# Two blocks of weights interleaved unit by unit while their turned operand is made

## The reference

```
h = rms_norm(x, norm_gain[i])            # first block; the even layer projects mem as well,
kv = einsum('bmd,dc->bmc', mem_n, w_kv)  # and keys and values of mem are two blocks of its columns
...
for l in range(DEPTH):                   # second block
    u = rms_norm_2(h, norm_pre_mix[l])
    p = (u @ w_in[l]).astype(jnp.float32)
    p_ret, p_hgrn, p_ml, p_rw = split_cols_2(p, GROUP_COLS)
    ...
    h = h + rms_norm_2(mixed, norm_post_mix[l])
    u = rms_norm_2(h, norm_pre_ffn[l])
    ffn = (jax.nn.silu(u @ w_ffn_gate[l]) * (u @ w_ffn_up[l])) @ w_ffn_down[l]
    h = h + rms_norm_2(ffn, norm_post_ffn[l])
```

## Time and profile before

| | us |
|---|---|
| median of 3 runs | 3916.73 (3912.31 to 3918.07) |
| span of the profiled execution | 3913.3 |
| TensorE busy | 3798.5 |
| VectorE busy | 2256.0 |
| ScalarE busy | 1795.6 |
| mean granted clock of TensorE | 0.985 |

### The profile page before, as it was taken

The page is one execution under the profiler, slowest core; times in us unless marked ns, Lnnn a source line. Parts: engine busy times, 40 slices in busy tenths (PEclk is TensorE's granted clock), DMA queues, the critical chain, the costliest instruction groups (busy, mean ns, idle before and its releaser), DMA issues.

```text
span 3913.3 us, 49190 instructions
## 1 busy us (share of the span) xinstructions
PE 3798.5 (97%) x19948; PEld 3204.6 (82%) x19948; DVE 2256.0 (58%) x3532; ACT 1795.6 (46%) x2519; POOL 104.5 (3%) x61
## 2 busy tenths in 40 slices
PE   8999999999999999989999999999999989999998
PEld 7886778787898897778888888988987778888887
DVE  5665666675555746764454444566656664445444
ACT  6454545445454424544444444545325454444443
POOL 0000000000010000000000000010000000000000
PEclk9999999999999999999999999999999999999999
DMA  7655546563554405446666655544225446666654
GB/s 239 184 167 147 145 135 179 158 188 101 182 165 135 122 26 159 146 146 190 191 188 189 200 194 193 178 125 143 63 78 153 152 140 189 192 189 189 201 193 169
DMA packets 341426, 628.34 MB, mean 161 GB/s; under 512 B 21088, under 2 KB 63024, under 8 KB 340432
## 3 DMA queue, kind: packets, MB, share of 16 engines
q1 hardware_dynamic: 331920, 611.53, 51.7%
q10 hardware_dynamic: 9280, 13.69, 1.1%
HBM read 623.04 MB, written 2.10 MB: 160 GB/s over the span
## 4 chain that ended last, share of the span: by engine, by line
PE 88%; DVE 6%; ACT 3%; POOL 1%; issue 1%; DMA 1%; SPq 0%; ACTq 0%; DVEq 0%; POOLq 0%
PE bank L621 74%; DVE weights_low L527 2%; PE bank L745 1%; PE bank L1320 1%; PE bank L1417 1%; PE bank L2524 1%; PE bank L2538 1%; PE bank L2131 1%; PE bank L2537 1%; ACT weights_high L514 1%; PE bank L600 1%; PE bank L1400 1%; POOL stat L706 0%; PE bank L1323 0%; POOL arena L706 0%
## 5 line engine op out<-in xcount | busy, mean ns | idle before, releaser
L527 DVE TENSOR_TENSOR weights_low<-weights,weights_high 128x1024 fp32r<-128x1024 f32 (+3 forms) x1176 | 1393.7, 1195 | 979.0 <-ACT weights_high L514 967.7
L514 ACT ACTIVATE weights_high<-weights 128x1024 fp32r<-128x1024 f32 (+3 forms) x1176 | 1206.9, 1030 | 1341.2 <-PE bank L621 1284.1
L621 PE MATMUL bank<-weights_high,x_high 128*128 128x512 f32 (+3 forms) x2816 | 1116.7, 397 | 21.4 <-DVE weights_low L527 9.7
L621 PE MATMUL bank<-weights_low,x_high 128*128 128x512 f32 (+3 forms) x2816 | 1086.3, 386 | 0.0
L621 PE MATMUL bank<-weights_high,x_low 128*128 128x512 f32 (+3 forms) x2816 | 1086.0, 386 | 0.0
L621 PEld LDWEIGHTS bank<-weights_high,x_high 128*128 128x128 f32 x2816 | 536.0, 190 | 135.4 <-DVE weights_low L527 17.2
L621 PEld LDWEIGHTS bank<-weights_low,x_high 128*128 128x128 f32 x2816 | 535.0, 190 | 101.8
L621 PEld LDWEIGHTS bank<-weights_high,x_low 128*128 128x128 f32 x2816 | 536.3, 190 | 93.1
L621 PE MATMUL bank<-x_high,weights_high 128*128 128x256 f32 x960 | 279.6, 291 | 12.2 <-DVE arena L650 6.0
L621 PE MATMUL bank<-weights_high,y_high 128*128 128x512 f32 (+1 forms) x672 | 266.2, 396 | 8.7 <-DVE weights_low L527 6.5
L621 PE MATMUL bank<-weights_high,ff_high 128*128 128x512 f32 x704 | 274.0, 389 | 0.0
(11 more groups left out here) (385 smaller groups left out, 3618.8 us busy)
## 6 DMA issues: line engine op xcount, KB each, us to landing
weights<-in_w_in_dram SPq DMA_DIRECT2D x208, 512.0 KB, 3.6
weights<-in_w_ffn_gate_dram SPq DMA_DIRECT2D x176, 512.0 KB, 3.7
weights<-in_w_ffn_up_dram SPq DMA_DIRECT2D x176, 512.0 KB, 3.6
weights<-in_w_ffn_down_dram SPq DMA_DIRECT2D x176, 512.0 KB, 3.6
weights<-in_w_out_dram SPq DMA_DIRECT2D x128, 512.0 KB, 3.6
weights<-in_even_w_in_dram SPq DMA_DIRECT2D x88, 512.0 KB, 3.6
weights<-in_odd_w_in_dram SPq DMA_DIRECT2D x80, 512.0 KB, 3.6
weights<-in_mem_w_kv_dram SPq DMA_DIRECT2D x32, 512.0 KB, 4.2
```

The costliest lines, as they stand in the source:

```text
L514: self.high_mark[g] = self.high_split.count(act.ran(nc.scalar.activation(high, raw, ACT.Copy)), act.clock)
L527: self.low_mark[g] = self.low_split.count(dve.ran(nc.vector.tensor_tensor(low, raw, high.bitcast(F32), ALU.subtract)), dve.clock)
L621: ins = pe.ran(nc.tensor.matmul(out, l, r, start=(u + c + x + y == 0), stop=(u == blk.n - 1 and c == UNIT - 1 and y == 1)))
```

## The change

`side_by_side(one, two)` takes the units of the two blocks added last and interleaves them: one's unit 0, two's unit 0, one's unit 1 and so on. It is called for mem0.k with mem0.v, o.i0 with o.i1, and in both layers of the second block for hgq with hgf0. For this the four chunks of hgf become two blocks of two chunks: hgf0 on banks 6 and 7, hgf1 on banks 4 and 5. Turns for these operands then use banks 4 and 5 alone (in `turn_x` with `spread`, and in `post_norm` after "down"). `hgrn` waits for three blocks in place of two. What is computed and every matmul is the same.

```diff
--- before.py
+++ after.py
@@ -485,6 +485,13 @@
         self.pair = 0
         self.add(Block(name, "features", self.by_unit(W, 0, D, col, chunks * P), D // (UNIT * P), chunks * P,
                        tuple(range(bank0, bank0 + chunks)), evac, AT, 0, None, scale))
+
+    def side_by_side(self, one, two):
+
+        n = self.blocks[one].n
+        first, second = self.units[-2 * n:-n], self.units[-n:]
+        assert {b.name for b, u in first} == {one} and {b.name for b, u in second} == {two}
+        self.units[-2 * n:] = [unit for both in zip(first, second) for unit in both]
 
     def load(self, g):
 
@@ -908,6 +915,8 @@
             for k, dst in ((0, self.mk[i]), (1, self.memv[i])):
                 self.tokens(f"mem{i}.{'kv'[k]}", self.hT_mem, A["mem_w_kv"][i], 0, D, k * 512, 512,
                             self.scaled_out(lambda t, dst=dst: dst[:, t, :], sc["mem"]), scale=sc["mem"])
+            if i == 0:
+                self.side_by_side("mem0.k", "mem0.v")
         self.plan_even()
         self.plan_odd()
         self.layers = [self.plan_layer(l) for l in range(2)]
@@ -978,6 +987,8 @@
                         self.scaled_out(lambda t: po[:, t, col:col + width], rs, ((0, width, func),)), scale=rs)
         for k in range(3):
             part(f"i{k}", 2560 + k * 368, 368)
+            if k == 1:
+                self.side_by_side("o.i0", "o.i1")
         part("k", O_["c_k"], 512)
         part("v", O_["c_v"], 512)
         for k in range(3):
@@ -1087,7 +1098,7 @@
                 yield
             self.ready([f"{name}{nb}"], self.pe)
             for c in (4 * nb, 4 * nb + 2):
-                self.turn(AT, c, self.x_chunk, 4 + c // 2 % 4, gain)
+                self.turn(AT, c, self.x_chunk, 4 + c // 2 % (2 if spread else 4), gain)
                 if nb < 3:
                     yield
         self.rms_of(self.squares, rs)
@@ -1739,8 +1750,10 @@
             dst = rows(HG + 2048 + k * 1024)
             self.tokens(n + "hg" + "ig"[k], L.hT, W, 0, D, (6 + k) * GW, GW,
                         self.scaled_out(lambda t, dst=dst: dst[:, t, :], L.pre, ((0, GW, func),)), scale=L.pre)
-        for k in range(2):
-            self.features(n + "hg" + "qf"[k], L.hT, W, 4 * GW + k * GW, 4, self.features_out(lambda j, k=k: room(HG, 4 * k + j), L.pre), 4 * k, scale=L.pre)
+        for name, col, chunks, at, bank in (("hgq", 0, 4, 0, 0), ("hgf0", GW, 2, 4, 6), ("hgf1", GW + 2 * P, 2, 6, 4)):
+            self.features(n + name, L.hT, W, 4 * GW + col, chunks, self.features_out(lambda j, at=at: room(HG, at + j), L.pre), bank, scale=L.pre)
+            if name == "hgf0":
+                self.side_by_side(n + "hgq", n + "hgf0")
         rwkv(0)
         rwkv(1)
         hgrn(0, ACT.Copy)
@@ -1891,7 +1904,7 @@
             if c == 0:
                 self.turn_first(AT, c, self.x_chunk, gain)
             else:
-                self.turn(AT, c, self.x_chunk, 4 + (c // 2 + 1) % 4, gain)
+                self.turn(AT, c, self.x_chunk, 4 + (c // 2 + 1) % (4 if "out" in name else 2), gain)
             if c == 0:
                 marks[2] = update(0, 2 * P, TILE)
                 if "out" in name:
@@ -2048,8 +2061,9 @@
         act.wait_ge(*[m for m in self.blocks["o.out_dsa3" if l == 0 else "0.down3"].done])
         for i, name in enumerate(("const_halves", "const_halves_T")):
             self.aux(masks[:, :, i, :], self.A[name].rearrange("p (l n) -> p l n", l=LEVELS))
-        yield from self.need(nm + "hgq", nm + "hgf")
-        self.ready([nm + "hgq", nm + "hgf"], act, dve)
+        names = [nm + "hgq", nm + "hgf0", nm + "hgf1"]
+        yield from self.need(*names)
+        self.ready(names, act, dve)
         yield from self.meet()
         landed = self.aux(gain, self.A["hgrn_norm_w_2"][l].partition_broadcast(P))
         over = lambda a: a.unsqueeze(2).broadcast_to([P, 4, S])
```

## The result

The changed kernel takes 3925.64 us (median of 6 runs, 3918.16 to 3930.57), the kernel before 3913.78 in the same job: a ratio of 1.0029, interval 1.0020 to 1.0039. It is slower, by 11.9 us. A later job with ten more runs of it gave 1.0027 (1.0018 to 1.0036). The forecast was 3917.6 in a range of 3904 to 3931, with 0.66 on "no difference" and 0.18 on slower. Its "no difference" reached 7.8 us to either side; 11.9 us lies outside it, on the slower side.

What follows compares the result with a forecast made beforehand. The prediction took TensorE, busy 3798.5 of 3913.3 us, as the bound. Its sum was 3916.7 - 0.1 (interleaving) + 1.0 (later hgrn chain) = 3917.6 us, all other terms 0; range 3904 to 3931 for 8 in 10.

Steps and rivals of the forecast that it cites:

- no difference: Case for the whole kernel: measured time within 7.8 us of no change, 3908.9 to 3924.6; chance 0.66.
- the four places: Where the change interleaves: TensorE already full while turns and stream alternate; gain taken 0.1 us, bound 1.7.
- A and B: Start (mem0.k, mem0.v) and first block of the odd layer (o.i0); gain taken 0 and 0.1 us.
- C: Start of layer 0 of the second block (hgq, hgf); interleaving gains 0 there.
- D: Start of layer 1 of the second block (hgq, hgf); interleaving gains 0 there.
- D's 4.1 and 0.7 us: Layer 1's start: TensorE waits for the first updated x and first low half; claimed to stay, gain 0.
- C's 0.9: Layer 0's start: TensorE's 0.91 us wait for an addition into x that frees bank 0; claimed to stay.
- Turns on two banks ... Taken 0: Layer 0 and 1 starts: a bank frees before the turn needing it; cost 0, up to 1 us possible.
- The chain behind the narrow units: hgrn's ACT chain behind hgf1 starts late through transfer waits; cost taken 1.0 us, 0 to 2.8 both layers.
- The slower rival: Behind hgf1, ACT's transfer waits become TensorE's through hgrn's chain: 13.5 us slower, 3930.2; chance 0.18.
- The faster rival: The shifted schedule frees the 3.41 us evacuation wait at 2750.95: 9.4 us gained, 3907.3, perhaps 3901.0; chance 0.16.
- The base: Starting time of the sum: 3916.7 us, the runs' median, 3.4 above the profiled span, carried unchanged.

Runs made afterwards that it cites:

- A and B alone: The kernel before with only mem0.k/mem0.v and o.i0/o.i1 interleaved; 3914.87 us, ratio 1.0001 (0.9992 to 1.0010).
- the change with its harm at C repaired: The changed kernel with three banks for the turns and the row of factors in layer 0 laid out later; 3916.22 us, ratio 1.0004 (0.9994 to 1.0015).
- two banks alone: The kernel before with turns in layers 0 and 1 on banks 4 and 5 in place of four, nothing interleaved or split; 3917.60 us, ratio 1.0012.
- second profile of the changed kernel: Another profiled execution of the changed kernel, same program; span 3921.9 us, against 3916.8 in the first profile.
- narrow units alone: The kernel before with hgf in two blocks of two chunks, nothing interleaved, four banks for the turns; 3916.01 us, ratio 1.0006 (0.9995 to 1.0016).
- three banks: The changed kernel with hgf0 cut to one chunk and hgf1 of three, leaving three banks for the turns; 3918.13 us, ratio 1.0008.
- layer 1 alone: The kernel before with only the change's layer 1 part: hgq and hgf0 interleaved, two banks for the turns; 3915.78 us, ratio 1.0004 (0.9996 to 1.0013).
- the late row: The changed kernel with layer 0's row of factors not laid out before the factor is expected, 27 weight matmuls ahead in place of 3; 3920.51 us, ratio 1.0012.
- early row: The kernel before with layer 0's row of factors laid out right behind the last turn, no weight matmul between; 3919.14 us, ratio 1.0008 (1.0000 to 1.0017).

## Why the prediction was right and wrong

- **The time lies in the range, the case doesn't.** 0.66 stood on a difference of less than 7.8 us, and it is 11.9. The range held because it was drawn wide for both rivals; neither made the difference.
- **That TensorE has nothing to fill at the four places** held. A and B alone give 1.0001, and the change with its harm at C repaired gains nothing. D's 4.1 and 0.7 us stayed, and C's 0.9 (now 0.7) nearly so, as the sum had them.
- **"Turns on two banks ... Taken 0" was the step that failed.** It rested on "each turn is followed by at least one unit". At C that wasn't so even in the kernel before, where only three matmuls of a unit's 24 stand between the last turns:

```profile
1060.10 0.60 PE L745 MATMUL bank<-const,x_residual 128*128 128x128 f32 x4
...
1060.89 0.60 PE L745 MATMUL bank<-const,x_residual 128*128 128x128 f32 x4
...
1061.68 1.04 PE L745 MATMUL bank<-const,x_residual 128*128 128x128 f32 x8
```

  With this order two banks alone cost a wait of 0.92 us, inside the 1 us that I allowed. But the order is computed anew from expected times, and the changed kernel has four turns in a row; its waits are 1.8. At D, where an update of x stands between turns, the wait for a bank is 0.2, though the row waits there too (0.2 in the change, 0.5 with two banks alone).
- **What hangs behind those turns had no term at all.** The row of factors was covered by 39 weight matmuls. With 3 in their place it costs 2.5 us of waiting, and the lower clock takes 2.6 more. Undoing this one thing gives 5.2 us back in C; making it in the kernel before costs 5.2. The sum never asks what the present order covers.
- **The chain behind the narrow units**, 1.0 us taken, at most 2.8, was right in kind in both layers. The sign is how far the chain's first table load on ACT stands ahead of rwr's last matmul: the later the chain, the longer DVE keeps the evacuation that rwk's first matmul waits for. Layer 0, ACT and then TensorE, in the kernel before and in the changed kernel:

```profile
1105.71 1.28 ACT L2062 ACT_TABLE_LOAD   x1
...
1126.58 0.28 PE L621 MATMUL bank<-x_high,weights_low 128*128 128x256 f32 x1
```

```profile
1116.12 1.28 ACT L2076 ACT_TABLE_LOAD   x1
...
1135.70 0.28 PE L628 MATMUL bank<-x_high,weights_low 128*128 128x256 f32 x1
```

  And layer 1, with the transfer that ACT waits for ahead of it:

```profile
2522.45 1.28 ACT L2059 ACT_TABLE_LOAD   x1
...
2543.32 0.28 PE L621 MATMUL bank<-x_high,weights_low 128*128 128x256 f32 x1
```

```profile
2531.30 1.06 ACT L521 ACTIVATE weights_high<-weights 128x1024 fp32r<-128x1024 f32 x1 [0.32 <-DMA weights<-in_w_in_dram]
...
2532.37 1.28 ACT L2073 ACT_TABLE_LOAD   x1
...
2552.56 0.28 PE L628 MATMUL bank<-x_high,weights_low 128*128 128x256 f32 x1
```

  The lead shrinks from 20.9 to 19.6 us in layer 0 and from 20.9 to 20.2 in layer 1, so the chain is 1.3 and 0.7 us late; the waits at rwk grow by 1.1 and 0.5. Together that is 1.6 us where 1.0 was taken (2.1 in the second profile of the changed kernel). The narrow units alone give the same in layer 0: 1.3 us late and the wait 1.1 longer. The rest of D's 1.8 us lies around the turns and the row (1.0) and in a little more time at the lower clock (0.4).
- **The slower rival** (13.5 us through those transfers) didn't come: ACT waited, TensorE hardly. The time that it named, 3930, is 4.6 us from the measured one, for another reason: it would be luck to count its 0.18 as a merit.
- **The faster rival** didn't come, but its mechanism did. The wait of 3.41 us at 2750.95 is there after the change, at 2762.77 and just as long. Of the two waits in layer 1's hgrn, though, that of 2.8 us is gone. In its place TensorE waits 1.5 us at 2643.89 and 0.7 at 2663.66, for evacuations and for DVE, which it didn't before. From rwk's first matmul to the wait of 3.41 us it takes 207.6 us, 205.5 before. The narrow units alone show the same waits and 207.5 us, so it is they that move the stalls, not the interleaving.
- **The base** was off by 3 us. The many runs of the kernel before have medians of 3913.8 to 3914.4 us. Each of them is some 1.5 us above its own span, so of the 3.4 us that I carried 1.5 were launch work and the rest was spread.

What stays open: why the order puts four turns in a row. Two banks alone bring the matmuls between last turn and row from 39 to 15, two banks with interleaving to 3, three banks with interleaving to 15, interleaving at A and B leaves 39. So both take part at C, but which expected time tips it wasn't tried. Open too is how much of D's 1.8 us, and of the 2 us behind it in layer 1, reaches the median: layer 1 alone gives 1.4 us, which can't be told from zero. And the late row gives back 3.8 us of the median (5.2 in C) in runs whose intervals touch, so its price in the median is known only roughly.

## What to carry to other kernels

Before buffers are shared out anew to let two streams run side by side, look at whether the stream has a gap there at all: if the engine is full, nothing can be gained, and what the streams take from (here banks for the turns) is a pure loss. Where a scheduler computes the order, a step that is covered now is covered by the present order alone; list for each wait that stands close to the edit what lies ahead of it, and count again in the new order. A wait costs more than itself if the matmul clock falls with it: here 2.5 us of waiting cost 2.6 more.

## What the runs showed of the hardware

- In the changed kernel TensorE's clock fell to 1.2 GHz after three waits of 0.5 to 0.7 us and within one of 2.5 (granted clock 0.54 over 1065 to 1072). With the same three waits without the fourth it held (the late row, 1.00), and so it did with 0.9 and 1.1 us (two banks alone, 1.00) and with one of 1.6 (three banks, 1.00). With a single wait of 3.4 us it held through the wait, fell when matmuls ran again and for less time (early row, 0.76 over the same 7 us).
- At the lower level matmuls of 256 columns start 0.21 us apart, at the higher 0.12.
- The same program's clock differs between executions: 0.98 and 0.94 over the same stretch of layer 1 (409 and 417 us), 8 us of time. A single profile can therefore hide a difference of 0.2%; stage by stage it is there.
- A narrow block's transfers of 256 KB land in 2.8 us and those of 512 KB in 3.7, in the changed kernel as in the one before (2.8 and 3.6). Sixteen narrow units in a row were enough for ACT to fall behind its loads by 4.2 us at once.
